# Attention on one Trainium2 core: where the operand splits stand between the 24 units, and where the exponential's table is loaded

## The reference

```
h = rmsnorm(x, g1) * (1 + sc1) + sh1
a_in, a_b, a_c, p_in, q, k, v = split(h @ w_in)          # 2560 columns
y = concat(conv(a_c * a_in) * a_b,                        # 256 columns
           pool(p_in),                                    # 256
           attention(q, k, v))                            # 512: 8 heads of 64
x = x + gt1 * (y @ w_out)                                 # 1024 x 1024
h = rmsnorm(x, g2) * (1 + sc2) + sh2
x = x + gt2 * peer(h)      # queries, top-k keys, 16384 experts' u and v
```

## Time and profile before

| | us |
|---|---|
| median of 3 runs | 2921.5 (2920.88 to 2922.55) |
| profiled execution | 2919.7 |
| its span, first to last instruction | 2917.9 |
| PE busy | 2857.4 (98%) |
| DVE busy | 1953.3 (67%) |
| ACT busy | 1241.8 (43%) |

### The profile page before, as it was taken

One profiled execution on the slowest core, in us unless ns is written; L12 is line 12 of the kernel. 1 busy time (PEld: TensorE's weight loads), 2 busy tenths in 40 slices (PEclk: granted clock), 3 DMA queues, 4 the chain that ended last, 5 costly groups with the idle time before them and its releaser, 6 DMA issues.

```text
span 2917.9 us, 43724 instructions
## 1 busy us (share of the span) xinstructions
PE 2857.4 (98%) x16094; PEld 2628.3 (90%) x16094; DVE 1953.3 (67%) x4289; ACT 1241.8 (43%) x2157; POOL 28.4 (1%) x57
## 2 busy tenths in 40 slices
PE   7999999999999999999999999999999999999998
PEld 6979999999999788888898799999999998888886
DVE  3545687877865588888665557778778755555555
ACT  3444434344344444444444453443433443444444
POOL 0000000000000000000000000000000000000000
PEclk9999999999999999999999999999999999999999
DMA  7452453854946977777542125448467398565662
GB/s 291 147 209 104 149 166 120 248 186 139 276 138 225 345 274 296 286 292 291 194 152 73 58 102 175 147 147 271 135 190 244 120 308 300 216 234 219 228 225 87
DMA packets 257487, 583.90 MB, mean 200 GB/s; under 512 B 13168, under 2 KB 210032, under 8 KB 212144
## 3 DMA queue, kind: packets, MB, share of 16 engines
q1 hardware_dynamic: 252192, 546.64, 54.7%
q0 software_dynamic: 5136, 35.14, 3.0%
HBM read 478.44 MB, written 103.29 MB: 199 GB/s over the span
## 4 chain that ended last, share of the span: by engine, by line
PE 94%; DMA 3%; DVE 1%; ACT 1%; issue 0%; SPq 0%; DVEq 0%; ACTq 0%
PE ps L839 35%; PE ps L879 34%; PE ps L691 11%; PE ps L861 6%; PE ps L713 2%; PE ps L804 1%; DMA gate_scratch<-g_all 1%; DMA act<-act_scratch 1%; PE ps L618 1%; PE ps L822 1%; PE ps L793 1%; PE ps L772 1%; DMA act_scratch<-act_h 1%; PE ps L659 1%; PE ps L771 0%
## 5 line engine op out<-in xcount | busy, mean ns | idle before, releaser
L839 PE MATMUL ps<-h_lo,u_hi 128*128 128x384 f32 x2048 | 693.1, 338 | 1.9 <-PE ps L822 1.0
L839 PE MATMUL ps<-h_hi,u_lo 128*128 128x384 f32 x2048 | 685.4, 335 | 0.0
L839 PE MATMUL ps<-h_hi,u_hi 128*128 128x384 f32 x2048 | 684.5, 334 | 0.0
L879 PE MATMUL ps<-v_lo,w_hi 128*128 128x512 f32 x1536 | 599.8, 391 | 6.1 <-DVE v_lo L1648 6.1
L879 PE MATMUL ps<-v_hi,w_hi 128*128 128x512 f32 x1536 | 598.5, 390 | 0.0
L879 PE MATMUL ps<-v_hi,w_lo 128*128 128x512 f32 x1536 | 598.5, 390 | 0.0
L1648 DVE TENSOR_TENSOR v_lo<-wring,v_hi 128x512 fp32r<-128x512 f32 x512 | 353.6, 691 | 317.0 <-ACT v_hi L1150 316.4
L1150 ACT CAST v_hi<-wring 128x512 fp32r<-128x512 f32 x512 | 317.1, 621 | 527.7 <-PE ps L879 527.4
L1507 DVE TENSOR_TENSOR u_lo<-wring,u_hi 128x1024 fp32r<-128x1024 f32 x256 | 313.0, 1223 | 178.4 <-ACT u_hi L1097 177.5
L839 PEld LDWEIGHTS ps<-h_lo,u_hi 128*128 128x128 f32 x2048 | 384.8, 188 | 2.9 <-DVE u_lo L1507 1.5
L839 PEld LDWEIGHTS ps<-h_hi,u_hi 128*128 128x128 f32 x2048 | 384.8, 188 | 0.0
(11 more groups left out here) (210 smaller groups left out, 3107.2 us busy)
## 6 DMA issues: line engine op xcount, KB each, us to landing
wring<-in_u_t_dram SPq DMA_DIRECT2D x128, 1024.0 KB, 5.7
wring<-in_v_t_dram SPq DMA_DIRECT2D x128, 1024.0 KB, 4.9
act_scratch<-act_h SPq DMA_DIRECT2D x256, 192.0 KB, 5.9
gate_scratch<-g_all SPq DMA_DIRECT2D x48, 1024.0 KB, 6.3
gate<-gate_scratch SPq DMA_DIRECT2D x64, 768.0 KB, 6.1
act<-act_scratch SPq DMA_DIRECT2D x64, 768.0 KB, 7.8
wring<-in_w_ada_dram SPq DMA_DIRECT2D x24, 1024.0 KB, 6.3
mod_w<-in_w_mod_dram POOLq DMA_DIRECT2D x24, 1024.0 KB, 7.0
```

The costliest lines, as they stand in the source:

```text
L839: last = nc.tensor.matmul(ps[:, 6 + s % 2, 0:T], u[:, s % 2, k], hx[:, k, 0:T], start=(k == 0 and n == 0), stop=(k == KC - 1 and n == 2))
L879: last = nc.tensor.matmul(ps[:, bank + tb], w[:, group * G + b, cols], v[:, n % 4], start=(first and n in (0, G) and k == 0), stop=(last_u ...
```

## The change

Pairs 0, 1 and 2 of y and the two weight pieces are split one at a time, at every third unit: on ScalarE at the end of n = 5, 8, 14 (y) and 17, 20 (weights), on VectorE at n = 6, 9, 15 and 18, 21, now behind the division of n-1. In layer 0 the modulation's last step on VectorE (n = 20) goes behind the division as well. A new one-column exponential stands in the last projection block of each layer, so the table is loaded there.

```diff
-OUT_AHEAD = 21
+Y_HIGH_AT, Y_LOW_AT = (5, 8, 14), (6, 9, 15)
+OUT_HIGH_AT, OUT_LOW_AT = (17, 20), (18, 21)
...
+        def exponent_table():
+
+            nc.scalar.activation(spare[:, 2:3], ones[:, 0:1], ACT.Exp)
...
                 if l and m == 0:
                     root(2 * l)
+                if m == 2 * N_IN - 1:
+                    exponent_table()
...
             for n in range(NU + 2):
-                if n == 0:
-
-                    act.wait_ge(branch_rdy.sem, branch_rdy.at(l, 1))
-                    high(l, 0, y, 0)
-                    high(l, 0, y, 1)
-                if n == OUT_AHEAD:
-                    columns_high(l, SP_OUT0)
-                    columns_high(l, SP_OUT0 + 1)
...
-                if n in (NU // 2 + 1, NU + 1):
-
-                    act.wait_ge(o_evac.sem, o_evac.at(l, n - 1))
-                    high(l, 0, y, 2 if n < NU else 3)
+                if n == Y_HIGH_AT[0]:
+                    act.wait_ge(branch_rdy.sem, branch_rdy.at(l, 1))
+                if n == Y_HIGH_AT[2]:
+                    act.wait_ge(o_evac.sem, o_evac.at(l, NU // 2))
+                if n == NU + 1:
+                    act.wait_ge(o_evac.sem, o_evac.at(l, NU))
+                if n in Y_HIGH_AT + (NU + 1,):
+                    high(l, 0, y, (Y_HIGH_AT + (NU + 1,)).index(n))
+                if n in OUT_HIGH_AT:
+                    columns_high(l, SP_OUT0 + OUT_HIGH_AT.index(n))
...
-                if l == 0 and n == ADA_TURN + 2:
-                    modulation(1, (4, 7), SC2, ROW_G2)
-                if n == 2:
-                    low(0, y, 0)
-                    low(0, y, 1)
-                if n == NU // 2 + 2:
-                    low(0, y, 2)
-                if n == OUT_AHEAD:
-                    columns_low(l, SP_OUT0)
-                    columns_low(l, SP_OUT0 + 1)
                 if n >= 1:
...
+                if l == 0 and n == ADA_TURN + 2:
+                    modulation(1, (4, 7), SC2, ROW_G2)
+                if n in Y_LOW_AT:
+                    low(0, y, Y_LOW_AT.index(n))
+                if n in OUT_LOW_AT:
+                    columns_low(l, SP_OUT0 + OUT_LOW_AT.index(n))
```

## The result

The changed kernel takes 2896.04 us (median of 4 runs, 2894.19 to 2898.37) against 2921.19 us for the kernel before (4 runs beside it, 2916.57 to 2922.55): ratio 0.9915, 95% interval 0.9901 to 0.9929. Forecast were 2897.0 us and a range of 2891.5 to 2905.

What follows compares the result with a forecast made beforehand. TensorE, busy 98% of the span, was taken as the bound, losing time in attention to waits and a lower clock. Layer 1's 16.3 plus layer 0's 8.35 gave 24.6 us off, so 2897 us, range 2891.5 to 2905.

Steps and rivals of the forecast that it cites:

- Part 1, the start: Start of attention, casts, table load and two splits moved away: 6.8 + 1.0 us gained in layer 1, 0.85 in layer 0.
- The step that names the table load: Before the first exponential: 1.28 us of table load leaves ScalarE's path, hidden in its 3.40 us wait before the last projection output.
- Part 2, pair 2: Split of y's pair 2 in mid-attention: moving it gains 3.9 us in layer 1 and 1.4 us in layer 0.
- Part 3, the weights at the end: Pair of weight splits at n = 21, end of attention: moving it gains 4.8 us in layer 1, 6.3 in layer 0.
- Part 4, the splits in their new places: Five single splits a layer behind the division: y's hidden, weights' 0.2 us late, so 0.2 us a layer charged.
- model turn: Layer 1's turn at 1597.74, used to price moved splits: y's split hidden by 0.2 us, a weight split 0.2 us late.
- At n = 18 the slack of the turns behind it takes that up: First weight split in attention: its 0.2 us of lateness is absorbed by later turns, so it costs nothing.
- The clock: TensorE's clock was expected to hold in attention; rival: it still falls at layer 1's start, 5.9 us, 2903 us, 9%.
- The slower rival: Each of five single splits costs as much as pair 2's did, with VectorE waiting for the cast: 2928 us, 3%.

Runs made afterwards that it cites:

- experiment 2: Changed kernel without the early table load, all splits moved: 2896.7 us, ratio 0.9923 to the kernel before.
- Experiment 4: Kernel before with only the two weight splits moved (ScalarE n = 17 and 20, VectorE n = 18 and 21, behind the division): 2910.56 us, ratio 0.9971.
- Experiment 12: Changed kernel with y's third pair and the first weight split exchanged (weight split at n = 15, y's at 18): 2900.65 us, ratio 0.9937 to the kernel before.
- experiment 3: Kernel before with unread matmuls filling TensorE's waits ahead of three transpositions of layer 1, splits unmoved: 2911.44 us, ratio 0.9963.
- experiment 5: Changed kernel with VectorE's single splits at the same units but ahead of the division: 2919.66 us, ratio 0.9998 to the kernel before.
- experiment 6: Changed kernel with each single split one unit earlier on both engines, still behind the division: 2902.6 us, ratio 0.9937 to the kernel before.
- experiment 7: Changed kernel with y's pairs 0 and 1 split together at n = 6 and both weights at n = 21: 2901.29 us, ratio 0.9935 to the kernel before.
- experiment 10: Changed kernel with the output projection's first three blocks of column 0 begun inside attention's last turns: 2893.87 us, ratio 0.9914 to the kernel before.

## Why the prediction was right

*Part 1, the start.* Layer 1: forecast 6.8 + 1.0. Heads 0 and 1 took 16.86 us before and 10.12 after, 6.74; head 2 went from 6.83 to 5.84, 0.99. The wait before tr(1) is 0.69 us (forecast 0.6), and tr(1) comes 4.77 us after the first scores (forecast 4.8). Layer 0: forecast 0.85, measured 0.92. The step that names the table load as part of this gain was too generous: it was removed from the path, but what was late next (the first maximum) would have hidden it in its old place, as experiment 2 shows. The sum did not depend on it, since I read the new time from the data's arrival and not from what was taken away.

*Part 2, pair 2.* Forecast 3.9 and 1.4. The two heads (4 and 5) gave 15.59 - 11.69 = 3.90 in layer 1 and 18.96 - 17.57 = 1.39 in layer 0.

*Part 3, the weights at the end.* Forecast 4.8 and 6.3; measured 15.22 - 10.44 = 4.78 and 16.79 - 10.44 = 6.35. Experiment 4 gets both from the weights alone.

*Part 4, the splits in their new places.* Forecast 0.2 us a layer, at n = 21, and nothing at n = 18. It is the other way round. Layer 1 pays at n = 18 and next to nothing at n = 21, layer 0 at neither. ScalarE, VectorE and TensorE of the changed kernel at the two places:

```profile
1599.88 0.48 ACT L1041 COPY prT<-ps 128x384 f32<-128x384 f32 x1 [0.15 <-PE ps L794]
1600.38 0.26 ACT L1048 COPY y<-ps 64x128 f32<-64x128 f32 x1
1600.67 1.05 ACT L951 CAST u_hi<-wring 128x1024 fp32r<-128x1024 f32 x1
1601.28 0.55 PE L794 MATMUL ps<-cst,pr 128*128 128x128 f32 x3
...
1601.75 1.23 DVE L1284 TENSOR_TENSOR u_lo<-wring,u_hi 128x1024 fp32r<-128x1024 f32 x1 [1.37 <-ACT u_hi L951]
...
1606.01 0.48 ACT L1041 COPY prT<-ps 128x384 f32<-128x384 f32 x1
1606.39 0.26 ACT L1048 COPY y<-ps 64x128 f32<-64x128 f32 x1
1606.55 1.05 ACT L951 CAST u_hi<-wring 128x1024 fp32r<-128x1024 f32 x1
1607.41 0.55 PE L794 MATMUL ps<-cst,pr 128*128 128x128 f32 x3
...
1607.63 1.23 DVE L1284 TENSOR_TENSOR u_lo<-wring,u_hi 128x1024 fp32r<-128x1024 f32 x1 [0.90 <-ACT u_hi L951]
```

At n = 18 the cast starts 0.61 us ahead of TensorE's transposition and the low split 0.47 behind it; at n = 21 it is 0.86 ahead and 0.22 behind. From one transposition to the next it takes 2.43 us with y's split at n = 15 (1595.43 to 1597.86), 2.55 at n = 21 (1607.41 to 1609.96) and 2.80 at n = 18 (1601.28 to 1604.08). So a weight split is 0.12 us late at n = 21 (0.2 was forecast), which does not show in the 10.44 us of the end, and 0.25 more at n = 18.

The 0.25 us are in the rows of ScalarE. The copy into y starts 0.50 us behind the copy of the probabilities at n = 17 and 0.38 at n = 20, and the cast 0.29 behind the copy into y against 0.16. The turns differ in the head whose result is copied: an odd one at n = 17, which goes to rows 64 to 127 of y, an even one at n = 20, which goes to rows 0 to 63. The longer pair of steps shows at odd heads and the shorter at even ones wherever ScalarE runs on without a wait, in layer 1 of both kernels and of every experiment. That the rows of y are the cause was not isolated. The prediction's model turn is an even one, here in the kernel before (its exponential at 1597.74 is in the earlier trace rows):

```profile
1597.58 0.26 ACT L1049 COPY y<-ps 64x128 f32<-64x128 f32 x1
```

My estimate took it for all five splits, and n = 18 is an odd one. Experiment 12 agrees: the weight split behind an even head's copy (n = 14) cost 0.13 us, and y's shorter split took the odd place without cost. "At n = 18 the slack of the turns behind it takes that up" is the step that failed: slack behind a stop of TensorE gives nothing back, because TensorE is the engine that sets the pace, and the head stayed at 6.22 us (5.84 + 0.38). The two errors, in size and in place, nearly cancel: 0.38 us in all against the 0.4 charged in both layers together. So the sum hides them: 24.6 forecast, 24.7 measured, and that closeness is in part luck.

*The clock.* That it held was the largest assumption. By experiment 3 it is worth 8.76 of layer 1's 16 us; by the windows of the two kernels it is 12.7 us of the whole gain. It held at 1.00 in six profiles of this start (the changed kernel three times, experiments 2, 5 and 12) and fell in three with the same order of work up to there (experiments 6, 7 and 10), at 3.1 to 3.2 us. The prediction put 5.9 us and 9% on it: too much in size, and by three of nine profiles too little in frequency. That the profiled execution shows none was in part luck; with one the time would have come out some 3 us higher, still inside the range. The Trainium skill (TensorE: Matmul & The Clock Gate, section A second HAM failure mode: psum-queue depth-cycling) names frequent short idle times as a cause of such swings. Between 1575 and 1607 us this trace does not bear it out for a TensorE that is idle for 1% of the time; at the start of layer 1, where the idle times are longer, it describes what some executions did.

*The slower rival.* Its mechanism is real ahead of the division (experiment 5, 2919.66 us) and absent behind it: there no wait of L794 exceeds 0.69 us. That is the reason that the prediction gives.

## What to carry to other kernels

Work that must share an engine with a chain goes behind the link that the busiest engine waits for, not ahead of it; with the splits spread over five units, that one line of order decided all 25 us here (experiment 5), and spreading alone brought none. The unit counts for less: the splits one unit earlier cost 6 us of it with the fall of the clock counted out (9.4 - 3.2 in the profile), in pairs 2.7 (5.8 - 3.1). When TensorE's waits are removed, price the clock too: compare its busy time over the stretch before with the same instructions' time where the clock stands at 1.00, since in this kernel the slow stretches behind the waits cost as much as the waits. And what is taken off a path is worth only what the next late thing leaves of it: the table load looked like 1.28 us a layer and was worth nothing.

## What the runs showed of the hardware

Whether the clock fell did not go by the length of the stop alone. The same 0.69 us before tr(1) let it stay at 1.00 in some executions and sent it to 0.50 for some 6 us in others. In layer 1's expert stage the changed kernel stood still for 2.49 us and went on at 1.00; TensorE's timeline and a window behind it:

```profile
2411.77 0.49 PE L880 MATMUL ps<-v_lo,w_hi 128*128 128x512 f32 x1 [2.49 <-DVE v_lo L1649]
```

```profile
2412.00:2418.00 6.00, 6.00 (x27) 1.00 1.04 409
```

In experiment 10 the stop at the same place was shorter, and the clock fell behind it:

```profile
2409.02 0.49 PE L894 MATMUL ps<-v_lo,w_hi 128*128 128x512 f32 x1 [1.98 <-DVE v_lo L1663]
```

```profile
2409.00:2415.00 6.00, 5.98 (x19) 0.72 1.03 404
```

How long it stays down varies as well: experiment 4's start of layer 1 stayed at 0.50 through three windows of 5 us, the kernel before for some 12 us, with the same splits there. Without the stops it did not fall: in experiment 3, where they were filled, layer 1 shows 1.00 throughout. What decides it behind a short stop is open; no run here isolates it.

The table load costs its 1.28 us and nothing behind it: in experiment 2 it ends at 1566.14 and the exponential starts at 1566.15, and in the earlier trace rows it starts 0.02 us behind the end of the casts. The Trainium skill (ScalarE: Activation LUTs, section What ACT_TABLE_LOAD costs) adds 1.38 us of drain to each; no such time shows in this trace.
